# Branch projections of a decoder layer as seven block products each, with the weight sums formed earlier and kept in DRAM

## The chip, the cores and the metric

One NeuronCore of a Trainium2 chip. The metric is the device time of one execution in microseconds; lower is better. TensorE (PE) multiplies, VectorE (DVE) and ScalarE (ACT) work beside it, SyncE (SP) and ACT issue the DMAs, each on a queue of its own. Each engine takes its instructions in order; waits on semaphores order them against each other.

## What is computed

One layer, 512 tokens, width 2048, float32. A normalised h feeds one wide input projection; 8 heads of three branches (differential attention, dilated attention, gated convolution) give three y of 512 x 1024. Then:

```python
gates = sigmoid(h @ w_gates + gate_b)            # 512 x 3 x 2048
merged = (gates[:, :, 0] * (ya @ w_branch_a)     # each 512x1024 @ 1024x2048
          + gates[:, :, 1] * (yb @ w_branch_b)
          + gates[:, :, 2] * (yc @ w_branch_c))
x = x + merged @ w_out                           # 512x2048 @ 2048x2048
out = rmsnorm(x) * final_g
```

## The kernel before

**Precision.** Each operand of a product is split into a high part (ACT, a copy to a rounded type, `hi_of`, line 705 on) and a low part (DVE, the difference, `lo_of`, line 1017). A product is three matmuls: high x high, low x high, high x low (`three`, lines 419 to 423). The profile's lines L421, L422 and L423 are these three, L703 and L707 ACT's splits, L1015 and L1019 DVE's.

**Weight ring.** Weights come in units of 128 x 1024 floats (512 KB) through a ring of three slots (`raw`, `w_hi`, `w_lo`). SP loads a slot when DVE has split the unit before in it (`ring_free`); ACT splits a unit when TensorE has used the one three places back; DVE follows; TensorE waits for DVE (`lo_done`).

**Stages.** (1) The heads: 8 heads x 18 blocks x 2 units of 24 matmuls, with attention in between. Beside this, once per head, ACT loads four quarters of w_out into `ssum` (block 2), DVE forms the sums of quarters (block 7, `sum_out_units`, line 1049), ACT stores them to `s_dram` (block 8). (2) The gates: the projection of h to 6144 columns in 6 quads of 1024 columns. A quad is a 2 x 2 block product in seven products instead of eight: sums of weight quarters (`add_units`, DVE) against sums of quarters of h (`t1` to `t4`, made by `combine_h` in the last head and in the first quad, with `f1` to `f4` as temporaries of 128 x 2048). A product has 4 units of 12 matmuls; a quad 28 units. The seven products accumulate in three pairs of PSUM banks (`CHAIN`, `FRESH`); DVE takes each into its outputs with the right sign (`take_g`). The gates go to `g_dram`. (3) The branches: 12 groups (3 branches x 4 groups of 512 columns), each 4 units of 24 matmuls, an ordinary product in one of two sets of four banks (`sets`). `load_gates` brings the four gate tiles of a group, DVE multiplies them in and adds into `merged` (`take_group`, lines 1370 to 1384). y comes from `y_dram` by `load_y` (2 MB) and is split in four pieces (`high_y`, `low_y`). For the last branch, merged is transposed by TensorE (`turn_merged`, line 631) and copied by ACT (`copy_merged`, line 911) into `m_t`. (4) The output: 2 quads of seven products of 4 units, as in the gates; the weight sums come from `s_dram`, those of merged are made in the first quad (`g1f`, `g3f`, `g4f`), x is loaded into `res` (line 957), and `take_o` (line 1415) evicts onto it.

The places of all this side work are written out by hand: in each engine's program, `if n == ...` after the split of unit n.

```python
for n in range(NU):                      # branches, DVE, before (abridged)
    lo_of(R_B + NU * g + n, ...)
    if n == 2:
        take_group(g - 1)
```

Of the kernel before, what the change touches and what calls it, by code (L numbers as in the profile page):

```python
# [27 lines left out]
P = 128  # L28
D = 2048
# [29 lines left out]
GROUPS, NU = 12, 4  # L59
R_G = W1  # L60
R_B = R_G + QUADS_G * STEPS
R_O = R_B + GROUPS * NU
X_B = 8 * QUADS_G
X_O = X_B + GROUPS * NU
W11, W12, W21, W22 = range(4)
ON_X, ON_Z, ON_Y = range(3)
# [7 lines left out]
S_ORDER = [2, 3, 0, 1]  # L74
# [11 lines left out]
def spot(s):  # L86
    return S_ORDER.index(s)
# [16 lines left out]
def program(nc, wst, wg, wb, wo, x_t, x_tok, cols_d, rows_d, lam_d, const_d, out_d):  # L104
# [4 lines left out]
    s_dram = nc.dram_tensor("s_dram", (HEADS, 4, P, HU), f32, kind="Internal").ap()  # L109

    with ExitStack() as ctx:
# [74 lines left out]
        with ExitStack() as c2:  # L186
            s2 = sb_in(c2)
            s2("below2", [P, KT * T])
# [14 lines left out]
        def part(tile, n):  # L203
# [12 lines left out]
        y_parts = [[tile[:, 4096 * n:4096 * (n + 1)].rearrange("p (k q) -> p k q", k=8) for n in at]  # L216
                   for tile, at in ((tb, (0, 1)), (kb_r, (1, 2)))] + [[act_hi[:, 0:8, :], act_hi[:, 8:16, :]]]
        y_raw = kb[:, 0:4096].rearrange("p (k q) -> p k q", k=8)
        merged = act_lo_f[:, :, :].rearrange("p (s k) q -> p s (k q)", s=4)

        m_t = tb_f[:, 0:8192].rearrange("p (k q) -> p k q", k=KT)
        flat_hi = act_hi[:, :, :].rearrange("p k q -> p (k q)")
        flat_gin = gin[:, :, :].rearrange("p k q -> p (k q)")
        o11 = [part(tb, 4), part(tb, 5)]
        o_t1, o_t2, o_t4 = [[part(kb_r, n), part(kb_r, n + 1)] for n in (0, 2, 4)]
        o_t3 = [part(gin_r, n) for n in (0, 1)]
        o21, o22 = [[part(flat_hi, n), part(flat_hi, n + 1)] for n in (0, 2)]
        operands_o = [o11, o_t1, o_t2, o21, o_t3, o22, o_t4]
        g1f, g4f, g3f = part(kb, 3), part(kb, 5), part(flat_gin, 1)
        m11, m12 = [m_t[:, 0:8, h * H:(h + 1) * H] for h in range(2)]  # L230
        m21, m22 = [m_t[:, 8:16, h * H:(h + 1) * H] for h in range(2)]
        res = merged

# [5 lines left out]
        sets = [sc_ps + tr_ps, [o_ps] + pb]  # L239
# [8 lines left out]
        yraw_in, gin_in = sem("yraw_in"), [sem(f"gin_in{i}") for i in range(2)]  # L248
# [21 lines left out]
        yhi_done, ylo_done = sem("yhi_done"), sem("ylo_done")  # L270
# [20 lines left out]
        def _(sp):  # L291
# [49 lines left out]
            def load_gates(g):  # L341
                b, cg = divmod(g, 4)
                sp.dma_start(gin[:, 4 * (g % 2):4 * (g % 2) + 4, :],
                             g_dram[b, :, :, C * cg:C * (cg + 1)].rearrange("s p q -> p s q")).then_inc(gin_in[g % 2], 16)
# [28 lines left out]
            sp.wait_ge(ylo_done, 4)  # L373
            load_y(1)
            for g in range(GROUPS):
                for u in range(NU):
                    ring_free(X_B + NU * g + u)
                    load_ring(X_B + NU * g + u, wb[g, u, :, :])
                    if g < 2 and u == 3:
                        for n in range(4 * g, 4 * g + 4):  # L380
                            sp.wait_ge(g_stored[n], 16 * QUADS_G)
                        load_gates(g)
                    if g >= 2 and u == 2:
                        if g < 6:
                            sp.wait_ge(m_got, 4 * (g - 1))
                        else:
                            sp.wait_ge(m_added, 4 * (g - 5))
                        load_gates(g)
                    if g == 2 and u == 0:
                        sp.wait_ge(ylo_done, 8)  # L390
                        load_y(2)
                    if g == 3 and u == 0:
                        sp.dma_start(rows[:, :], rows_d[0:1, 3 * D:4 * D].to_broadcast([P, D])).then_inc(grow_in, 16)
            for q in range(QUADS_O):
                for n in range(STEPS):
                    p, u = divmod(n, NU)
                    x = X_O + STEPS * q + n
                    ring_free(x)
                    load_ring(x, wo[NU * q + u, (W11, None, None, W12, None, None, W22)[p], :, :] if p in (0, 3, 6) else
                              s_dram[NU * q + u, (None, W22, W11, None, W21, W12, None)[p], :, :])  # L400
# [15 lines left out]
        def _(pe):  # L416
# [176 lines left out]
            def product(r, operand, banks, p, free=None, between=None):  # L593

                hi, lo = operand
                for u in range(NU):
                    pe.wait_ge(lo_done, r + NU * p + u + 1)
                    slot = (r + NU * p + u) % RING
                    for s in range(2):
                        if free and u == 0:  # L600
                            pe.wait_ge(free[0], free[1][s])
                        for kk in range(2):
                            k, ts, cs = 2 * u + kk, slice(P * s, P * (s + 1)), slice(C * kk, C * (kk + 1))
                            end = three(banks[s][:, :], hi[:, k, ts], lo[:, k, ts], w_hi[slot][:, cs], w_lo[slot][:, cs],
                                        FRESH[p] and k == 0, k == 7, True)
                    end.then_inc(pe_used, 1)
                    if between:
                        between(u)
# [11 lines left out]
            for q in range(QUADS_G):  # L620
                for p in range(PRODUCTS):
                    if q == 0 and p in (1, 2, 4):
                        pe.wait_ge(comb_lo, {1: 1, 2: 2, 4: 4}[p])
                    product(R_G + STEPS * q, operands_g[p], pairs[(q + CHAIN[p]) % 3], p, free_g(q, p))

            def turn_merged(g, s):

                cg = g % 4
# [939 lines left out]
```

## Time and profile before

| | us |
|---|---|
| median of 3 runs (2642.91 to 2644.52) | 2642.93 |
| the profiled execution's own time | 2641.48 |
| its span | 2639.7 |
| TensorE busy / DVE busy / ACT busy | 2616.3 / 1554.9 / 866.8 |
| mean granted clock of TensorE | 0.997 |

Stages on TensorE, by the first matmul of each: heads from 8.8, gates from 1735.2, branches from 2203.3, output from 2469.9; the last matmul starts at 2628.6. "Busy" counts a matmul to its modelled end, and matmuls overlap; their rate is read from the starts.

### The profile page before, as it was taken

Reading aid. Unit: us, or ns where it says so; the run is one execution under the profiler, and the core shown is the slowest. Engines: PE = TensorE matmul, PEld = TensorE weight load, DVE = VectorE, ACT = ScalarE, POOL = GpSimd, SP = SyncE. Lnnn points to the kernel's source line nnn. Section 1 sums busy time; section 2 is a strip of 40 time slices with the busy share of each in tenths; the row PEclk is TensorE's granted clock in tenths of the full one; section 3 lists DMA queues with packets and bytes.
Section 4 is the critical chain, followed back from the end, with each engine's and each line's share of the span. In section 5 each row is a group of like instructions: output and inputs, shape, how many; then the busy total and the mean of one; then the engine's idle time right before and its main releaser. Section 6 shows DMA issues by size and latency. Waiting matters only on the chain.

```text
span 2639.7 us, 31265 instructions
## 1 busy us (share of the span) xinstructions
PE 2616.3 (99%) x12030; PEld 2162.5 (82%) x12030; DVE 1554.9 (59%) x1911; ACT 866.8 (33%) x1089; POOL 0.2 (0%) x4
## 2 busy tenths in 40 slices
PE   9999999999999999999999999999999999999998
PEld 7888888888888888888888888878888888888776
DVE  7653654554455455365455446798877784444775
ACT  6222332322222233232232223334444443212454
POOL 0000000000000000000000000000000000000000
PEclk9999999999999999999999999999999999999999
DMA  6333333332332432333334243435455436444565
GB/s 220 120 92 126 97 118 97 120 124 91 124 132 84 131 116 89 112 108 123 93 120 131 84 132 124 139 114 186 168 190 177 164 131 247 160 144 143 189 190 195
DMA packets 102825, 359.41 MB, mean 136 GB/s; under 512 B 10017, under 2 KB 10274, under 8 KB 100770
## 3 DMA queue, kind: packets, MB, share of 16 engines
q1 hardware_dynamic: 82352, 296.49, 34.2%
q10 hardware_dynamic: 20338, 60.89, 6.3%
q8 instruction: 113, 1.85, 0.3%
q14 instruction: 22, 0.18, 0.0%
HBM read 317.50 MB, written 39.85 MB: 135 GB/s over the span
## 4 chain that ended last, share of the span: by engine, by line
PE 95%; DVE 3%; DMA 1%; issue 1%; SPq 0%; ACT 0%; DVEq 0%; ACTq 0%
PE proj L421 22%; PE proj L423 22%; PE proj L422 22%; PE sc_ps L421 3%; PE sc_ps L422 3%; PE sc_ps L423 3%; PE tr_ps L421 3%; PE tr_ps L422 3%; PE tr_ps L423 3%; PE o_ps L422 2%; PE o_ps L423 2%; PE o_ps L421 2%; PE tr_ps L462 2%; PE sc_ps L454 1%; DVE w_lo L1019 1%; PE o_ps L507 1%
## 5 line engine op out<-in xcount | busy, mean ns | idle before, releaser
L421 PE MATMUL proj<-act_hi,w_hi 128*128 128x512 f32 x2304 | 908.1, 394 | 0.5 <-DVE stage L1146 0.2
L423 PE MATMUL proj<-act_hi,w_lo 128*128 128x512 f32 x2304 | 898.2, 390 | 0.0
L422 PE MATMUL proj<-act_lo,w_hi 128*128 128x512 f32 x2304 | 897.2, 389 | 0.0
L1015 DVE TENSOR_TENSOR w_lo<-raw,w_hi 128x1024 fp32r<-128x1024 f32 x288 | 352.7, 1225 | 396.4 <-ACT w_hi L703 395.9
L703 ACT ACTIVATE w_hi<-raw 128x1024 fp32r<-128x1024 f32 x288 | 304.6, 1058 | 837.3 <-PE proj L423 832.3
L423 PEld LDWEIGHTS proj<-act_hi,w_lo 128*128 128x128 f32 x2304 | 432.5, 188 | 91.4
L421 PEld LDWEIGHTS proj<-act_hi,w_hi 128*128 128x128 f32 x2304 | 432.8, 188 | 89.2 <-issue 1.1
L422 PEld LDWEIGHTS proj<-act_lo,w_hi 128*128 128x128 f32 x2304 | 433.0, 188 | 86.3
L1019 DVE TENSOR_TENSOR w_lo<-raw,w_hi 128x1024 fp32r<-128x1024 f32 x152 | 185.7, 1223 | 219.2 <-ACT w_hi L707 218.9
L707 ACT ACTIVATE w_hi<-raw 128x1024 fp32r<-128x1024 f32 x152 | 161.2, 1061 | 353.3 <-PE proj L423 149.9
L707 ACT ACTIVATE w_hi<-kb 128x1024 fp32r<-128x1024 f32 x120 | 127.2, 1061 | 185.8 <-PE proj L423 65.4
L1019 DVE TENSOR_TENSOR w_lo<-kb,w_hi 128x1024 fp32r<-128x1024 f32 x120 | 146.5, 1222 | 57.5 <-ACT w_hi L707 57.5
L770 ACT ACTIVATE sc<-sc,nmax 128x768 f32<-128x768 f32 (+4 forms) x96 | 65.5, 683 | 181.2 <-DVE nmax L1160 101.1
L1146 DVE TENSOR_TENSOR stage<-proj,rstd 128x512 f32<-128x512 f32 x40 | 27.6, 691 | 97.8 <-PE proj L423 97.8
L421 PE MATMUL tr_ps<-w_hi,act_hi 128*128 128x512 f32 x192 | 74.7, 389 | 0.0
L422 PE MATMUL tr_ps<-w_lo,act_hi 128*128 128x512 f32 x192 | 74.7, 389 | 0.0
L784 ACT ACTIVATE qk_hi<-stage 128x512 fp32r<-128x512 f32 x32 | 20.2, 632 | 150.1 <-DVE stage L1146 106.2
L421 PE MATMUL sc_ps<-w_hi,act_hi 128*128 128x512 f32 x160 | 63.0, 394 | 2.5 <-DVE w_lo L1019 2.5
L1144 DVE TENSOR_TENSOR stage<-proj,rstd 128x512 f32<-128x512 f32 x24 | 26.1, 1088 | 64.6 <-PE proj L423 64.6
L422 PE MATMUL sc_ps<-w_lo,act_hi 128*128 128x512 f32 x160 | 63.0, 394 | 0.0
L421 PE MATMUL sc_ps<-w_hi,tb 128*128 128x512 f32 x144 | 56.4, 392 | 1.5 <-issue 1.5
L421 PE MATMUL proj<-w_hi,act_hi 128*128 128x512 f32 x144 | 56.3, 391 | 1.2 <-DVE w_lo L1019 1.2
(297 smaller groups left out, 3354.5 us busy)
## 6 DMA issues: line engine op xcount, KB each, us to landing
raw<-wst SPq DMA_DIRECT2D x288, 512.0 KB, 3.5
raw<-wg SPq DMA_DIRECT2D x48, 512.0 KB, 4.0
raw<-wb SPq DMA_DIRECT2D x48, 512.0 KB, 3.6
kb<-wg SPq DMA_DIRECT2D x10, 2048.0 KB, 7.6
ssum<-wo ACTq DMA_DIRECT2D x8, 2048.0 KB, 10.5
s_dram<-ssum ACTq DMA_DIRECT2D x8, 2048.0 KB, 7.5
raw<-s_dram SPq DMA_DIRECT2D x32, 512.0 KB, 3.4
kb<-wg SPq DMA_DIRECT2D x24, 512.0 KB, 5.9
```

Of the source, the lines that this page charges most:

```text
L421: nc.tensor.matmul(out, w_h, a_h, start=first, stop=False, skip_group_check=shared)
L422: nc.tensor.matmul(out, w_h, a_l, start=False, stop=False, skip_group_check=shared)
L423: return nc.tensor.matmul(out, w_l, a_h, start=False, stop=last, skip_group_check=shared)
L454: end = nc.tensor.matmul(sc_ps[m][:, 0:n], q_part[AQ][rows, qs], k_part[AK][rows, 0:n], start=step == 0, stop=step == 2)
L462: end = nc.tensor.transpose(tr_ps[idx % 2][:, n * P:(n + 1) * P], tile, ident[:, :])
L507: nc.tensor.matmul(o_ps[:, c * P:(c + 1) * P], v_g[g][:, c, :], pt_g[:, g - 1, c, :], start=g == 1 and c == 0, stop=False)
L703: nc.scalar.activation(w_hi[slot_w][:, :], raw[slot_raw][:, :], ACT.Copy).then_inc(hi_done, 1)
L707: nc.scalar.activation(w_hi[r % RING][:, :], src, ACT.Copy).then_inc(hi_done, 1)
L770: end = nc.scalar.activation(tile[:, lo:hi], tile[:, lo:hi], ACT.Exp, scale=scale, bias=nmax[:, m:m + 1], accum_out=sums[:, m:m + 1])
L1015: tt(w_lo[slot_w][:, :], raw[slot_raw][:, :], w_hi[slot_w][:, :].bitcast(f32), ALU.subtract).then_inc(lo_done, 1)
L1019: tt(w_lo[r % RING][:, :], src, w_hi[r % RING][:, :].bitcast(f32), ALU.subtract).then_inc(lo_done, 1)
L1146: ins = tt(blk[w][:, :], pb[w % RING][:, :], rstd[:, :], ALU.mult)
```

## The change

- Branches: 6 quads (`QUADS_B`) of 1024 columns, each a 2 x 2 block product with seven products of 2 units of 12 matmuls (`STEPS_B` = 14 units), in the order P1, P2, P6, P5, P7, P3, P4 (`ORDER_B`), in the three bank pairs. The first use of an output is copied by ACT from PSUM to `parts` (`first_of`), the second added by DVE; then the gates are multiplied in and merged is added to (`finish`, `finish_last`, `gate`).
- y: seven operands per branch, four of them sums of quarters made by DVE (`sum_y`), each split into high and low. The loads of y stand at units 9 of quad 0 and 6 of quad 2.
- Weight sums for branches and output (20 in all, `SUMMED`) are formed in blocks 2, 7 and 10 of the heads 0 to 6 (head 0 without block 2), loads in blocks 1, 4, 9, stores in 3, 8, 11. Branch and output weights are one array `ws`.
- `load_gates` brings the two tiles of one output part, at units 5, 7, 9 and 12.
- The sums of h: `f1`, `f2` earlier in the last head, `f4` and a three-step `f3` in the first gate quad; two of the first weight sums in block 16.
- Output: `m_t` lies where act_hi was; merged parts of the last quads are transposed one at a time through the fourth bank pair; x is loaded at unit 7 instead of 6; the row of final_g during the output's first quad.

```diff
-GROUPS, NU = 12, 4
+QUADS_B, STEPS_B, NU = 6, 14, 4
+P1, P5, P6, P2, P7, P3, P4 = range(PRODUCTS)
+ORDER_B = [P1, P2, P6, P5, P7, P3, P4]
+SLOT = {0: 0, 3: 0, 1: 1, 2: 1}
+GATED = [0, 3, 1, 2]
+LOAD_AT, SUM_AT = {1: 0, 4: 1, 9: 2}, {2: 0, 7: 1, 10: 2}
...
@@ SP @@
-            sp.wait_ge(ylo_done, 4)
-            load_y(1)
...
+            for qb in range(QUADS_B):
+                for n in range(STEPS_B):
+                    load_unit(X_B + STEPS_B * qb + n, 2 * qb + n % 2, ORDER_B[n // 2])
+                    if qb == 0 and n == 0:
+                        load_gates(0, 0)
+                    if n == 5:
+                        load_gates(qb, 3)
+                    if n == 7:
+                        load_gates(qb, 1)
+                    if n == 9:
+                        load_gates(qb, 2)
+                    if n == 12 and qb < QUADS_B - 1:
+                        load_gates(qb + 1, 0)
+                    if (qb, n) == (0, 9):
+                        sp.wait_ge(ylo_done, 6)
+                        load_y(1)
+                    if (qb, n) == (2, 6):
+                        sp.wait_ge(ylo_done, 7 + 6)
+                        load_y(2)
...
@@ PE @@
+            def turn_merged(qb, d):
+                pair = qb % 2
+                for s in range(2):
+                    n = gated(qb - 4, d, s)
+                    pe.wait_ge(m_added, gated(qb - 2, d, s))
+                    if n > 2:
+                        pe.wait_ge(m_copied, n - 2)
...
+            for qb in range(QUADS_B):
+                for i, p in enumerate(ORDER_B):
+                    if qb % 2 == 0:
+                        pe.wait_ge(ylo_done, 7 * (qb // 2) + i + 1)
+                    product(R_B + STEPS_B * qb + 2 * i, operands_y[qb // 2][p], pairs[(QUADS_G + qb + CHAIN[p]) % 3], p,
+                            free_b(qb, p), turns_b(qb, 2 * i), 2)
+            def turns_o(u):
+                if u in (0, 1, 3):
+                    turn_merged(5, {0: 3, 1: 1, 3: 2}[u])
...
@@ ACT @@
+            FIRST_AT = {4: P1, 8: P6, 10: P5}
...
-                    if q == 0 and n in (5, 6):
...
-                    if q == 0 and n == 6:
+                    if q == 0 and n == 2:
+                        first_of(QUADS_B - 1, P4)
+                    if q == 0 and n in (4, 5, 7):
+                        copy_merged(5, {4: 3, 5: 1, 7: 2}[n])
+                    if q == 0 and n == 7:
                         for i in range(4):
...
@@ DVE @@
+            def finish(qb, p):
+                d, first, op = {P2: (0, P1, ALU.add), P7: (3, P5, ALU.subtract), P3: (1, P6, ALU.add)}[p]
+                dve.wait_ge(pe_used, RING + R_B + STEPS_B * qb + 2 * ORDER_B.index(p) + 2)
+                bank = pairs[(QUADS_G + qb + CHAIN[p]) % 3]
+                for s in range(2):
+                    dve.wait_ge(d_first, first_in(qb, first, s))
+                    tt(parts[2 * SLOT[d] + s], parts[2 * SLOT[d] + s], bank[s][:, :], op).then_inc(d_added, 1)
+                dve.wait_ge(d_added, added_in(qb, p, 1))
+                gate(qb, d)
...
+                    elif n == 0:
+                        finish(qb - 1, P3)
+                    elif n == 3:
+                        finish_last(qb - 1)
+                    if n == 6:
+                        finish(qb, P2)
+                    if n == 12:
+                        finish(qb, P7)
+                    if qb in (1, 3):
+                        b = (qb + 1) // 2
+                        if n in (1, 4, 5, 7):
+                            sum_y(b, (P5, P6, P7, P4)[(1, 4, 5, 7).index(n)])
+                        if n in (8, 9, 10, 11, 13):
+                            low_y(b, (8, 9, 10, 11, 13).index(n))
+                    if qb in (2, 4) and n in (1, 4):
+                        low_y(qb // 2, 5 if n == 1 else 6)
```

## Rows read from the trace of the kernel before

**Rows 1.** The page, part 1: busy us (share of the span) x instructions.
```profile
PE 2616.3 (99%) x12030; PEld 2162.5 (82%) x12030; DVE 1554.9 (59%) x1911; ACT 866.8 (33%) x1089; POOL 0.2 (0%) x4
```

**Rows 2.** Busy time of each engine in two stretches, first gates, then output.
```profile
core 0: us, PE busy (x) PEld busy (x) DVE busy (x) ACT busy (x) POOL busy (x), PEclk, DMA share, GB/s
1820.00:2120.00 300.00, 300.00 (x1325) 248.51 (x1324) 238.70 (x229) 132.39 (x140) 0.00 (x0) 1.00 0.50 172
...
2530.00:2620.00 90.00, 90.00 (x399) 74.53 (x398) 57.58 (x62) 41.14 (x53) 0.00 (x0) 1.00 0.62 194
```

**Rows 3.** TensorE's waits, longest first: us in total, times, longest us.
```profile
PE sc_ps L421 <- DVE act_lo_f L1415: 2.5, 1, 2.5
PE sc_ps L421 <- DVE w_lo L1019: 2.5, 1, 2.5
```

**Rows 4.** Last head and first gate quad: timeline of DVE, of TensorE, and a stretch.
```profile
1720.24 1.23 DVE L1015 TENSOR_TENSOR w_lo<-raw,w_hi 128x1024 fp32r<-128x1024 f32 x1 [5.99 <-ACT w_hi L703]
...
1730.37 4.63 DVE L1033 TENSOR_TENSOR kb<-kb 128x1024 f32<-128x1024 f32 x4
...
1747.10 0.63 PE L422 MATMUL sc_ps<-w_lo,act_hi 128*128 128x512 f32 x1
1747.52 0.63 PE L423 MATMUL sc_ps<-w_hi,act_lo 128*128 128x512 f32 x1
...
1735.20:1787.00 51.80, 46.91 (x188) 36.57 (x187) 50.85 (x44) 20.99 (x19) 0.00 (x0) 0.93 0.25 80
```

**Rows 5.** Busy time over the whole branch stage (columns as in rows 2).
```profile
2203.30:2469.90 266.60, 266.57 (x1201) 221.51 (x1202) 119.47 (x134) 70.83 (x74) 0.00 (x0) 1.00 0.48 162
```

**Rows 6.** Heads 4 and 5: timeline of DVE and ACT; DMA issues (KB, us to landing).
```profile
997.20 1.23 DVE L1015 TENSOR_TENSOR w_lo<-raw,w_hi 128x1024 fp32r<-128x1024 f32 x1 [2.67 <-ACT w_hi L703]
1001.55 0.69 DVE L1146 TENSOR_TENSOR stage<-proj,rstd 128x512 f32<-128x512 f32 x1 [3.12 <-PE proj L423]
...
1106.02 1.06 ACT L703 ACTIVATE w_hi<-raw 128x1024 fp32r<-128x1024 f32 x1 [3.13 <-PE proj L423]
...
1117.99 1.23 DVE L1015 TENSOR_TENSOR w_lo<-raw,w_hi 128x1024 fp32r<-128x1024 f32 x1 [2.37 <-ACT w_hi L703]
...
DMA to landing us min/median/max: 8.2/10.5/10.7
...
s_dram<-ssum ACTq DMA_DIRECT2D x8, 2048.0 KB, 7.5
```

**Rows 7.** Start of the branches: timelines of SP, ACT, DVE and TensorE.
```profile
2188.35 0.43 SPq L339 DMA_DIRECT2D kb<-y_dram  x1
2190.70 12.89 SPq L312 DMA_DIRECT2D raw<-wb  x4
...
2193.79 1.06 ACT L707 ACTIVATE w_hi<-raw 128x1024 fp32r<-128x1024 f32 x1 [1.66 <-PE proj L423]
2200.92 1.06 ACT L707 ACTIVATE w_hi<-raw 128x1024 fp32r<-128x1024 f32 x1 [6.06 <-DMA raw<-wb]
...
2202.01 1.22 DVE L1019 TENSOR_TENSOR w_lo<-raw,w_hi 128x1024 fp32r<-128x1024 f32 x1 [5.90 <-ACT w_hi L707]
...
2203.33 0.47 PE L421 MATMUL sc_ps<-w_hi,tb 128*128 128x512 f32 x1 [1.48 <-issue]
```

**Rows 8.** Branches: additions into merged on DVE; DMA issues of units and gates.
```profile
2317.14 2.49 DVE L1384 TENSOR_TENSOR act_lo_f<-act_lo_f,gin 128x512 f32<-128x512 f32 x4
...
raw<-wb SPq DMA_DIRECT2D x48, 512.0 KB, 3.6
...
gin<-g_dram SPq DMA_DIRECT2D x12, 1024.0 KB, 5.9
```

**Rows 9.** Output's start: two stretches, TensorE's timeline, landing of the four x loads.
```profile
2469.90:2530.00 60.10, 56.40 (x254) 45.62 (x253) 52.15 (x45) 33.30 (x33) 0.00 (x0) 1.00 0.65 227
...
2482.00:2502.00 20.00, 17.48 (x81) 14.26 (x80) 16.44 (x14) 10.95 (x10) 0.00 (x0) 1.00 0.98 377
...
2496.10 0.47 PE L421 MATMUL sc_ps<-w_hi,kb_r 128*128 128x512 f32 x1 [2.52 <-DVE act_lo_f L1415]
...
DMA to landing us min/median/max: 7.4/13.6/19.1
```

More of the change, by code:

```diff
@@ L232, in program @@
         res = merged
+        parts = [rows[:, C * n:C * (n + 1)] for n in range(4)]
         pb = [ctx.enter_context(nc.psum_tensor(f"proj{i}", [P, T], f32)) for i in range(RING)]
@@ L590, in _, with product @@
                 blocks(i, 0)
-            def product(r, operand, banks, p, free=None, between=None):
+            def product(r, operand, banks, p, free=None, after=None, nu=NU):
                 hi, lo = operand
-                for u in range(NU):
-                    pe.wait_ge(lo_done, r + NU * p + u + 1)
-                    slot = (r + NU * p + u) % RING
+                for u in range(nu):
+                    pe.wait_ge(lo_done, r + u + 1)
+                    slot = (r + u) % RING
                     for s in range(2):
@@ L621, in _ @@
                 for p in range(PRODUCTS):
[L622 to L628, printed above, removed]
-                pe.wait_ge(m_added, 4 * (g - 4) + spot(s) + 1)
-                for kk in range(4):
-                    end = nc.tensor.transpose(sets[g % 2][s][:, P * kk:P * (kk + 1)],
-                                              merged[:, s, C * cg + P * kk:C * cg + P * (kk + 1)], ident[:, :])
-                end.then_inc(m_turned, 1)
@@ new lines, in _ @@
+                    product(R_G + STEPS * q + NU * p, operands_g[p], pairs[(q + CHAIN[p]) % 3], p, free_g(q, p))
+            def turn_merged(qb, d):
[5 more added lines that the diff above has]
+                        pe.wait_ge(m_copied, n - 2)
+                    c0 = C * (2 * pair + d // 2)
+                    for kk in range(4):
+                        end = nc.tensor.transpose(pairs[3][s][:, P * kk:P * (kk + 1)],
+                                                  merged[:, 2 * (d % 2) + s, c0 + P * kk:c0 + P * (kk + 1)], ident[:, :])
+                    end.then_inc(m_turned, 1)
@@ L1378, in take_group, with gate @@
+            def gate(qb, d):
+                b, cg = qb // 2, 2 * (qb % 2) + d // 2
+                dve.wait_ge(gin_in[d], 16 * (qb + 1))
+                for s in range(2):
+                    to, tile = merged[:, 2 * (d % 2) + s, C * cg:C * (cg + 1)], gin[:, 2 * d + s, :]
+                    stt(to if b == 0 else tile, tile, 1.0, parts[2 * SLOT[d] + s], ALU.add, ALU.mult).then_inc(m_got, 1)
                 if b:
[L1379 to L1381 removed]
+                    for s in range(2):
+                        to, tile = merged[:, 2 * (d % 2) + s, C * cg:C * (cg + 1)], gin[:, 2 * d + s, :]
+                        dve.wait_ge(m_got, gated(qb, d, s))
```

468 lines of the change are left out of this document (251 added, 217 removed).

## The prediction

> **What bounds the kernel now.** I read the page first: TensorE is busy for 2616.3 us of a span of 2639.7 us, DVE for 1554.9, ACT for 866.8 [rows 1]. The profiled execution took 2641.48 us, 1.8 us more than its span and 1.45 us under the median of 2642.93; I sum against the execution and move the difference to the median. A busy TensorE need not be a fast one, so I took windows without a wait: the first of [rows 2] has 1325 matmuls in 300.00 us, a pitch of 0.2264 us (the 0.39 us of a row is latency, not rate). A unit of 12 matmuls is then 2.72 us, one of 24 is 5.43 us. The list of TensorE's waits is short; its two longest are 2.5 us each [rows 3]. So time falls only with fewer matmuls, if no other engine then holds TensorE up.
>
> How much room is there? The ring has three slots. ACT's split of a unit starts 0.2 us after the unit three places back has ended, DVE's split 1.1 us after ACT's (2200.92, 2202.01), and TensorE can begin 1.3 us after that (2203.33) [rows 7]. Of the two units between, 5.4 us, some 2.6 us are used and **2.8 us are left** when units have 12 matmuls; with 24 it is 8.3 us. DVE spends 1.14 us on 1024 elements (four in 4.63 [rows 4]); ACT's 128x1024 I take at 1.0.
>
> **The change, part by part.**
>
> 1. *Fewer matmuls.* A branch had 4 groups x 4 units x 24 = 384 matmuls; now 2 quads x 7 products x 2 units x 12 = 336. Three branches: 1152 less 1008 = 144, all 128x512. 144 x 0.2264 = **-32.6 us**. The transposes of the merged sum stay 64. The stage took 266.6 us for 1201 matmuls [rows 5], as the pitch says, so nothing else is hidden in it.
>
> 2. *Weight sums in the heads.* 20 in place of 8, each a load of 2 MB, four DVE adds (4.6 to 4.8 us together) and a store. Today's, in block 7, hold up no matmul: none of the waits lies in the heads [rows 3]. At block 10 they come behind the split at 997.20 and end at 1003.1; the eviction stood at 1001.55, so it and what follows slip 1.6 us, under 8.3. At block 2 they follow the split at 1117.99 and shift what is behind them as little. The load for block 2 is issued behind ACT's split at 1106.02 and lands at the worst in 10.7 us [rows 6], at 1116.9, 2.3 us early; that of block 9 stands equally far ahead of block 10's sums. The store before a load takes 7.5 us [rows 6] of the 10.9 that a block gives it. Cost taken **0**; bounds: nothing, and, if a load under the added 48 MB lands 8 us late, 1 to 2 us in each of 13 places.
>
> 3. *Sums of h, last head and first gate quad.* DVE is solid there from 1730.37 on (50.85 us of the window's 51.80 [rows 4]), and the window's 188 matmuls would do with 42.6: 9.2 us lost, some 3 of them to matmuls at twice the pitch (1747.10 to 1747.52; granted clock 0.93 in the window [rows 4]). The change takes two add units (2.3) and both operations on f4 (4.5) out of blocks 16 and 17, puts the adds into an idle DVE (5.99 us before 1720.24 [rows 4]), and brings f4 (two) and a third f3 operation back inside the quad, f4's last two at 17 and 20. Going instruction by instruction with 1.14, 2.2 (2048 wide) and 1.32 us (two evictions), TensorE waits 0.4 at unit 3, 1.9 at 4, 1.8 at 5, and 0.3 to 1.3 at 7, 9, 10, 12, 14 and 15: 8.3 us. **-1 us**, bounds -4 and +3.
>
> 4. *Start of the branches.* Today the 2 MB load of branch 2's y (2188.35) goes ahead of the first branch unit (2190.70), whose split starts at 2200.92 rather than one unit behind those at 2193.79, at 2196.5; TensorE idles 1.48 us [rows 7]. This load moves: **-1.5**.
>
> 5. *The two loads of y.* They now stand in the middle of quads 0 and 2, where units last 2.72 us. In [rows 7] the unit behind the y load was there 12.6 us after that load's issue (2188.35 to 2200.92). Counting from a quad's first matmul, SP issues the y load of quad 2 at 5.5 (after DVE's split 3), so unit 7 is there at 18.1, where ACT wants it at 2.72 x 5 + 0.2 = 13.8: 4.3 late, less 2.8 of room, 1.5. In quad 0 the load goes out at 14.1 behind a gate load (0.5 MB, about 1 us): unit 10 at 27.7 against 22.0, less 2.8: 2.9. I add 0.8 for the units that follow, whose room is spent: **+5.2**. Bounds: 0, if a unit lands in its usual 3.6 us [rows 8] all the same, and 9.
>
> 6. *DVE in the branches.* A quad lasts 38.1 us. Splits take 14 x 1.14 = 15.9. An operation on 128x512 takes 0.60 to 0.62 us (four in 2.49 [rows 8]): a finish is two adds, two gatings, two sums into merged and its waits, 3.8; three of these and the last (2.5) make 13.9. Quad 3 adds four sums and five low parts of y, 10.2: **40.0 in 38.1**. Split n can begin at 2.72(n - 2) + 1.3 and must by 2.72n - 1.3. From quad 3's split 6 at 13.0 the DVE queue has no gap: finish to 18.0, split 7 at 18.0 (0.3 late), then with sums and low parts split 9 at 22.6, 11 at 27.1, 12 at 29.4, finish to 34.4, split 13, a low part, split 0 of quad 4 at 36.6, finish(P3) to 41.6, and split 1 there, due at 39.5: **+2.1**. After it there is time. Quad 1 has no sums into merged (34.8) and passes. Quad 5 has g1f and two low parts, 2.2 us each, at units 10, 11 and 13: its split 13 begins at 34.7 (0.6 late), split 0 of the output stage at 38.0 (1.2 late in all), and split 1, behind finish(P3), at 43.0; both are counted in the next term. ACT has 14 splits and 7 high parts at 1.0 and 8 copies, taken at DVE's 0.6: 26 us of 38, room.
>
> 7. *Start of the output stage.* Today TensorE lost 4.5 us in it: 254 matmuls, 16 of them transposes (about 1.8), in 60.10 us, against 55.6; the largest piece is 2.52 us before 2496.10, on the eviction of the first product behind 2048-wide DVE work [rows 9]. In the new order the transpose of quad 5's part 1 follows unit 1, but its bank is emptied by ACT behind the split of unit 4, which waits for unit 1: 1.0 and two copies, 1.9 us of idle TensorE. The copies of part 2 move from unit 6 to 7, and behind them the x load and the split of the third operand. On that clock of quad 5 (stage due at 38.1): unit 0 at 39.3, unit 1 at 44.3, unit 2 at 49.7, unit 7 done at 66.9. ACT splits unit 7 at 58.8, copies, and has the third operand's high part at 63.4; DVE's low part 65.6, split 8 66.8, the next operand's low part 69.0, split 9 70.2, first eviction 71.5. Product 3 may start then, at 71.6; without any loss it would start at 38.1 + 8 x 2.72 + 2.6 for 24 transposes = 62.5. So 9.1 us are lost against today's 4.5 to 4.8: **+4.3**, bounds 0 and 8. The x load's first quarter took 7.4 us [rows 9]; issued at 59.5 it is there at 67, before DVE asks.
>
> 8. *Traffic.* Unit loads double to 193 GB/s, gates 55, y 18: 266 GB/s. The chip moved 377 GB/s over 20 us [rows 9], and the output stage runs at 194 with TensorE never idle, 90.00 us of 90 [rows 2]. **0** beyond term 5. The gate loads moved later are each issued four or more units (11 us) ahead of use, and took 5.9 us for twice the bytes [rows 8].
>
> Sum: -32.6 - 1 - 1.5 + 5.2 + 2.1 + 4.3 = **-23.5 us**; 2641.5 becomes 2618.0, the median 2642.9 becomes **2619**.
>
> **A rule beside this.** After one of the 2.5 us waits the matmuls from 1747.10 ran 0.42 us apart, the 1.2 GHz level; after 2.52 us at 2496.10 the stretch kept a granted clock of 1.00 [rows 4, 9]. Terms 5 to 7 make some six new waits of 1 to 3 us; a slow stretch costs 7 x 0.2 = 1.4 us by those rows.
> The Trainium skill (TensorE: Matmul & The Clock Gate, Part 1) says that activity is what holds the clock up and that idleness gives it back to half rate, which speaks against any change that breaks up an unbroken stream. By that rule all six waits would be followed by such a stretch; by the row at 2496.10, none.
>
> **Rivals.**
> A. *Nothing new is exposed.* The y loads hold nothing up and DVE keeps pace: terms 5 to 7 vanish, 2643 - 35 = 2608; with half of term 7, 2610. For it: DVE is busy for only 119.47 of today's 266.60 us of branches [rows 5]. Against: the quads' sums above. 0.15.
> B. *More waits than I see.* Late ring units, DVE lateness and the slow clock fall together: 6 x 1.4 = 8 us, or double terms 5 and 7: 2627 to 2632. For it: twice the load rate, 2.8 us of room. 0.2.
> C. *The branches become DMA-bound, slower than before.* 84 units of 0.52 MB, 12.6 MB of gates and 4.2 of y are 61 MB. If the queue sustained only the 194 GB/s of the output stage, the stage would take 314 us, 47 longer: about 2692. It decides below 236 GB/s (258 us). Against: 377 GB/s in [rows 9]. 0.04.
> D. *The products don't shrink*, or a loss about equal to the gain: within 0.2%. The loops give 84 units of 12. 0.03.
> The forecast has 0.58.
>
> **Numbers.** 0.2% is 5.3 us, about what a measurement of this kernel can tell from no change. Faster: forecast, A and B, 0.93; same 0.03; slower 0.04. The range runs from A's 2608, less 2 for the bound of term 3, to the greater part of B, 2630.
>
> **What would show it.** TensorE: 11886 matmuls, busy less by 28 to 33 us. By step: waits on a raw unit in quads 0 and 2; a wait on DVE's split in quad 4's first units; an idle of 2 us before a transpose early in the output stage, and one of about 5 us on the first output eviction; no wait at the branches' first unit; no new one in the heads. I am wrong if the heads show TensorE waiting on DVE or ACT on ssum, or if unit loads in the branches come over 5 us after issue throughout.

## The result and the profile after

The changed kernel takes **2630.11 us** (median of 4 runs, 2625.20 to 2632.15) against 2643.72 beside it: ratio 0.9945 [0.9928, 0.9963], 13.6 us less. Run again later it took 2629.85 against 2644.85, ratio 0.9945 [0.9928, 0.9961]. It is faster, as forecast, but by 14 us where the forecast said 23.5; 2630.11 lies at the far end of the range (2606 to 2630), 0.1 us past it. The two profiled executions differ by 9.3 us (2632.15 and 2641.48). The one of the changed kernel is the slowest of its four; the fastest took 2625.20 us at a mean granted clock of 0.997, the other three had 0.995.

In the changed kernel L464 to L466 are the three matmuls, L752 ACT's split, L1097 DVE's, L679 the transposes of merged, L983 ACT's copies of them, L1491 the adding of a branch product and L1544 the output's eviction; the variants below shift these numbers by a few lines. The page of the changed kernel, part 1, stands against [rows 1]:

```profile
PE 2593.7 (99%) x11886; PEld 2138.7 (81%) x11886; DVE 1700.2 (65%) x2053; ACT 936.7 (36%) x1182; POOL 0.2 (0%) x4
```

144 matmuls fewer, as the sum said, and TensorE's busy time is 22.6 us less, not 28 to 33. Stage by stage (the same windows as [rows 2], the first gate quad as in [rows 4], the branch stage as in [rows 5], the first 60 us of the output stage as in [rows 9]):

```profile
core 0: us, PE busy (x) PEld busy (x) DVE busy (x) ACT busy (x) POOL busy (x), PEclk, DMA share, GB/s
1820.00:2120.00 300.00, 300.00 (x1325) 248.41 (x1324) 238.82 (x229) 133.14 (x142) 0.00 (x0) 1.00 0.51 172
1738.60:1790.40 51.80, 45.92 (x191) 34.80 (x191) 50.29 (x43) 19.20 (x18) 0.00 (x0) 1.00 0.23 77
2204.40:2451.70 247.30, 238.49 (x1049) 194.77 (x1048) 200.71 (x222) 137.70 (x163) 0.00 (x0) 0.99 0.73 248
2451.70:2512.00 60.30, 52.57 (x223) 41.70 (x224) 46.81 (x41) 30.32 (x30) 0.00 (x0) 0.94 0.65 228
```

The gates run as before. The branch stage has 152 matmuls fewer than [rows 5] and is only 19.3 us shorter, not 34; the output's first 60 us hold 223 matmuls instead of 254. These are TensorE's waits from the branches on; the kernel before has two long ones there, 1.48 us ahead of the first branch unit [rows 7] and 2.52 us at the output's first eviction [rows 9]:

```profile
engine line waited for: us in total, times, longest us
PE tr_ps L464 <- DVE w_lo L1097: 5.2, 3, 3.7
PE sc_ps L464 <- DVE act_lo_f L1544: 4.0, 1, 4.0
PE sc_ps L464 <- DVE w_lo L1097: 2.8, 2, 2.5
PE proj L679 <- ACT act_hi_f L983: 2.0, 1, 2.0
PE o_ps L464 <- DVE w_lo L1097: 1.4, 2, 1.1
PE sc_ps L464 <- DVE rows L1491: 1.0, 1, 1.0
```

The waits are not the whole loss. Below is the timeline of TensorE in quad 0 of the branches, then two windows, one behind the wait there and one behind that of the first eviction:

```profile
2235.52 0.47 PE L464 MATMUL tr_ps<-w_hi,kb_r 128*128 128x512 f32 x1 [3.72 <-DVE w_lo L1097]
...
2237.14 0.63 PE L464 MATMUL tr_ps<-w_hi,kb_r 128*128 128x512 f32 x1
2237.57 0.63 PE L465 MATMUL tr_ps<-w_lo,kb_r 128*128 128x512 f32 x1
```
```profile
2235.50:2241.00 5.50, 5.48 (x17) 4.40 (x18) 4.85 (x6) 1.84 (x3) 0.00 (x0) 0.69 0.79 232
2484.90:2489.00 4.10, 4.09 (x12) 3.27 (x13) 2.79 (x4) 0.00 (x0) 0.00 (x0) 0.63 1.00 405
```

From 2236.74 eight matmuls start 0.43 us apart instead of 0.2264: the granted clock is at its 1.2 GHz level after the wait, and TensorE is busy at half the rate. Such a stretch costs 8 x 0.2 = 1.6 us, 1.65 with its ends, and there are four: behind the waits of 3.72, 2.50, 1.95 and 4.02 us.

To compare kernels I summed, over TensorE's timeline, what each start lies beyond 0.2267 us after the one before it, in groups of at least 0.3 us. "Gates" is the first gate quad, "quads" are the waits on ring units in quads 0 to 3 with what follows them, "DVE" what the branches lose to a late DVE, "output" begins with the last units of quad 5. The last but one column is the first matmul of the gate stage.

| | gates | quads | DVE | output | start of gates | median |
|---|---|---|---|---|---|---|
| before | 9.2 | 1.7 | 0 | 4.5 | 1735.2 | 2643.7 |
| after | 8.5 | 9.9 | 2.5 | 13.1 | 1738.7 | 2630.1 |
| after, again | 8.5 | 12.0 | 1.9 | 12.8 | 1735.6 | 2629.9 |
| y whole, on ACT's queue | 8.6 | 4.8 | 1.5 | 10.7 | 1738.2 | 2624.4 |
| y in two blocks | 8.5 | 3.5 | 2.1 | 11.1 | 1735.8 | 2622.1 |
| y in four pieces | 8.6 | 0 | 2.1 | 12.6 | 1735.6 | 2619.5 |
| + transposes later | | 1.7 | 2.0 | 9.7 | 1738.2 | 2616.0 |
| + eviction earlier | | 0.6 | 2.0 | 12.4 | 1735.9 | 2618.9 |
| + x taken apart | | 1.3 | 2.1 | 8.7 | 1736.8 | 2616.9 |
| + DVE relieved | | 1.3 | 4.2 | 11.2 | 1735.9 | 2620.2 |
| without the branches' weight sums | 8.5 | 13.4 | 1.5 | 12.0 | 1740.3 | 2629.5 |
| all that helped | 8.5 | 0.3 | 2.0 | 2.3 | 1735.9 | 2608.8 |

(The lines with + build each on the four pieces. The last column is the median of four runs, the others come from one profiled execution each. The medians stem from four measurements, the last three on three different chips, each beside the kernel before, whose own median went from 2643.4 to 2644.9; ratios below are to it, and their intervals reach 4 to 5 us either way, so differences of 3 us between variants are indications.) For the two profiled executions the table gives -32.6 for the matmuls, -0.7, +8.2, +2.5, +8.6 and +3.5 for the start, so -10.5; the spans differ by -9.4.

### The profile page after: what moved, and what is told of

It is laid out like the page before. It is cut to its first block, busy times and chain, and to the rows that moved or that the text cites. A ratio compares the mean times of both kernels' runs of the same rounds, so it can differ in the third digit from the quotient of the medians.

```text
span 2630.3 us, 31503 instructions
## 1 busy us (share of the span) xinstructions
PE 2593.7 (99%) x11886; PEld 2138.7 (81%) x11886; DVE 1700.2 (65%) x2053; ACT 936.7 (36%) x1182; POOL 0.2 (0%) x4
## 4 chain that ended last, share of the span: by engine, by line
PE 89%; DVE 5%; DMA 3%; ACT 1%; issue 1%; SPq 0%; ACTq 0%; DVEq 0%
PE proj L464 21%; PE proj L466 21%; PE proj L465 21%; PE tr_ps L464 3%; PE tr_ps L466 3%; PE tr_ps L465 3%; PE sc_ps L464 3%; PE sc_ps L466 3%; PE sc_ps L465 3%; DMA raw<-s_dram 2%; DVE w_lo L1097 2%; PE tr_ps L505 2%; PE o_ps L465 2%; PE o_ps L466 2%; PE o_ps L464 2%
## 5 line engine op out<-in xcount | busy, mean ns | idle before, releaser
L464 PE MATMUL proj<-act_hi,w_hi 128*128 128x512 f32 x2304 | 908.8, 394 | 0.2 <-DVE stage L1219 0.2
L466 PE MATMUL proj<-act_hi,w_lo 128*128 128x512 f32 x2304 | 899.0, 390 | 0.0
L748 ACT ACTIVATE w_hi<-raw 128x1024 fp32r<-128x1024 f32 x288 | 305.0, 1059 | 826.2 <-PE proj L466 819.9
L1093 DVE TENSOR_TENSOR w_lo<-raw,w_hi 128x1024 fp32r<-128x1024 f32 x288 | 352.6, 1224 | 375.9 <-ACT w_hi L748 374.5
L466 PEld LDWEIGHTS proj<-act_hi,w_lo 128*128 128x128 f32 x2304 | 432.8, 188 | 91.4
L464 PEld LDWEIGHTS proj<-act_hi,w_hi 128*128 128x128 f32 x2304 | 433.2, 188 | 88.7 <-issue 1.6
L1097 DVE TENSOR_TENSOR w_lo<-raw,w_hi 128x1024 fp32r<-128x1024 f32 x188 | 229.2, 1223 | 119.0 <-ACT w_hi L752 118.7
L752 ACT ACTIVATE w_hi<-raw 128x1024 fp32r<-128x1024 f32 x188 | 199.5, 1062 | 265.8 <-PE tr_ps L466 69.4
L752 ACT ACTIVATE w_hi<-kb 128x1024 fp32r<-128x1024 f32 x120 | 127.5, 1062 | 186.4 <-PE proj L466 66.7
L1097 DVE TENSOR_TENSOR w_lo<-kb,w_hi 128x1024 fp32r<-128x1024 f32 x120 | 146.8, 1224 | 51.8 <-ACT w_hi L752 51.7
L464 PE MATMUL sc_ps<-w_hi,tb 128*128 128x512 f32 x200 | 79.9, 399 | 4.3 <-DVE w_lo L1097 3.2
L464 PE MATMUL tr_ps<-w_hi,tb 128*128 128x512 f32 x200 | 78.5, 393 | 4.7 <-DVE w_lo L1097 4.6
L466 PE MATMUL sc_ps<-w_hi,tb 128*128 128x512 f32 x200 | 79.3, 396 | 0.0
L465 PE MATMUL sc_ps<-w_lo,tb 128*128 128x512 f32 x200 | 79.2, 396 | 0.0
L466 PE MATMUL tr_ps<-w_hi,tb 128*128 128x512 f32 x200 | 77.9, 389 | 0.0
L465 PE MATMUL tr_ps<-w_lo,tb 128*128 128x512 f32 x200 | 77.9, 389 | 0.0
```

What stands on the lines that cost most here:

```text
L464: nc.tensor.matmul(out, w_h, a_h, start=first, stop=False, skip_group_check=shared)
L465: nc.tensor.matmul(out, w_h, a_l, start=False, stop=False, skip_group_check=shared)
L466: return nc.tensor.matmul(out, w_l, a_h, start=False, stop=last, skip_group_check=shared)
L748: nc.scalar.activation(w_hi[slot_w][:, :], raw[slot_raw][:, :], ACT.Copy).then_inc(hi_done, 1)
L752: nc.scalar.activation(w_hi[r % RING][:, :], src, ACT.Copy).then_inc(hi_done, 1)
L1093: tt(w_lo[slot_w][:, :], raw[slot_raw][:, :], w_hi[slot_w][:, :].bitcast(f32), ALU.subtract).then_inc(lo_done, 1)
```

## Experiments

### The changed kernel again

No edit.

> The changed kernel, unaltered, beside three variants of it. Question: are the extra 3 us ahead of the gates (start of the gates at 1738.65 instead of 1735.2) and the four stretches at half the TensorE clock behind long waits (at 2236.74, 2308.46, 2462.13 and 2485.92) a property of the program, or of one execution? If of the program: gates start at 1738 to 1739 again, and the same four waits are each followed by some 8 matmuls at 0.43 us, 1.65 us lost each. If of the execution: the start lies near 1735.5 and some of the four stretches are missing. Median near 2630 either way.

Measured: 2629.85 us (2629.43 to 2632.81). The first 60 us of the first execution, and of this one:

```profile
0.00:60.00 60.00, 56.46 (x259) 46.93 (x260) 40.65 (x69) 35.17 (x53) 0.20 (x4) 0.97 0.54 193
```
```profile
0.00:60.00 60.00, 57.38 (x277) 47.19 (x278) 42.49 (x71) 36.98 (x56) 0.20 (x4) 1.00 0.56 198
```

The same program started its gates at 1738.65 once and at 1735.58 once: the 3 us ahead of the gates belong to the execution. What separates the two is a wait of TensorE near 40 us, on an early sum of DVE, and a slow stretch behind the longer one:

```profile
40.33 1.02 PE L577 MATMUL tr_ps<-ones,xacc 128*128 128x1 f32 x8 [1.53 <-DVE xacc L1151]
```
```profile
38.99 1.02 PE L577 MATMUL tr_ps<-ones,xacc 128*128 128x1 f32 x8 [0.30 <-DVE xacc L1151]
```

No part of the change makes it. The expectation had tied both questions together, and they came out apart: the four slow stretches came back at the same four waits, the first of them with some 13 slow matmuls instead of 8. In these two executions of one program they stand in the same places. How far that holds for a changed one, the run with ACT's queue shows.

### y of branches 1 and 2 in four pieces

The edits from here on are shown abridged.

```
-  if (qb, n) == (0, 9): load_y(1)        # 2 MB
-  if (qb, n) == (2, 6): load_y(2)
+  if n in (8, 10, 11, 13) and qb in (0, 2): load_y_part(1 + qb // 2, ...)   # 0.5 MB
-  wait_ge(yraw_in, 16 * (b + 1))
+  wait_ge(yraw_in, 16 * (4 * b + 1))
```

> The loads of y of branches 1 and 2, 2 MB each, are cut into four pieces of 0.5 MB, issued on SP's queue at units 8, 10, 11 and 13 of quads 0 and 2 instead of all at once at unit 9 of quad 0 and unit 6 of quad 2. Nothing else is changed. Theory (the load as one block holds up the ring's unit behind it, and the wait is paid twice, once as itself and once as a stretch at half the clock): the waits of 3.72 us (quad 0) and 2.50 us (quad 2) fall to under 0.5 us each and the half-clock stretches behind them (1.65 us each) go with them, so 8 to 9.5 us less than the changed kernel, about 2621. Rival 1 (the bytes themselves are the limit, the same 2 MB beside the ring's units): the waits are spread into several small ones with the same sum, and only the half-clock stretches may go: 0 to 3.3 us less. Rival 2 (the half clock has to do with something else than the wait ahead of it): the waits go, the slow stretches stay: 6 us less.

Measured: 2619.45 us (2618.53 to 2619.76), ratio 0.9902 [0.9885, 0.9918]; 10.4 us less than the changed kernel beside it. TensorE's waits in the branches, all of them:

```profile
engine line waited for: us in total, times, longest us
PE tr_ps L469 <- DVE w_lo L1102: 1.2, 1, 1.2
PE sc_ps L469 <- DVE w_lo L1102: 0.3, 1, 0.3
```

Theory held, rivals 1 and 2 fell: the same bytes, in pieces between the ring's units, cost TensorE nothing, and the slow stretches of these two places went with the waits. What is left are the two of DVE.

### y whole, but on ACT's queue

```
-  sp.dma_start(y_raw, ...)      # unit 9 of quad 0, unit 6 of quad 2
+  act.dma_start(y_raw, ...)     # behind ACT's unit 7 and unit 4
```

> The loads of y of branches 1 and 2 stay whole (2 MB) but are issued by ACT on its own queue, behind its high parts of unit 7 of quad 0 and unit 4 of quad 2, at about the same moments as before. If order within one queue is what delays the ring's unit (it may not pass the 2 MB in front of it), the unit lands in 4 to 7 us after its issue instead of 11.7 to 12.6, and the waits of 3.72 and 2.50 us on PE fall under 1 us: 5 to 9 us less than the changed kernel. If it is the bandwidth of the moment (both queues share the same engines) the waits stay within 1 us of what they are, and the time is the same within 3 us.

Measured: 2624.43 us (2622.01 to 2625.34), 5.4 us less than the changed kernel. The size fits the first reading, but not the rows. The wait in quad 0, in this kernel, and the windows behind it and behind the first eviction:

```profile
2234.24 0.47 PE L458 MATMUL tr_ps<-w_hi,kb_r 128*128 128x512 f32 x1 [2.92 <-DVE w_lo L1095]
```
```profile
2234.20:2239.70 5.50, 5.46 (x24) 4.55 (x25) 4.83 (x6) 2.25 (x3) 0.00 (x0) 1.00 0.83 272
2476.70:2481.00 4.30, 4.26 (x19) 3.54 (x20) 2.82 (x4) 0.00 (x0) 0.00 (x0) 1.00 1.01 407
```

The wait in quad 0 is 0.8 us shorter, not gone (quad 2 loses 1.7 us, where the changed kernel lost 2.7 and a slow stretch). Order in one queue would have had the unit land 4 to 7 us after its issue; it landed after 9.9 us, against 10.6 in the changed kernel. In its own queue the unit did pass the load (it landed at 2231.80, y at 2235.40), yet ACT could split it at 2231.83, against 2233.10, and of this gain 0.5 us are the earlier start of this execution and some may be the earlier issue of the load (2219.60, against 2221.45). So order is not the main cause, at least in quad 0; in quad 2, where the load went out 2.7 us earlier than before, the wait fell by more, from 2.50 to 1.01 us. What is left is that the load's bytes and the ring's share the same transfer engines. In the changed kernel's trace these have no room while the unit is awaited (slices of a fortieth of 2226 to 2233; the share of the 16 engines is 9 tenths or more throughout):

```profile
DMA  9999999999999999999999999999999999999999
...
DMA packets 1156, 2.83 MB, mean 404 GB/s; under 512 B 41, under 2 KB 41, under 8 KB 1156
```

The Trainium skill (DMA: Bandwidth & Descriptors, Where 436 GB/s comes from) puts the side of the HBM at some 358 GB/s for one core; these 404 GB/s are above it, and nearer to the 425 that the same page gives for a load of 16 MB with one core at work.
The same trace has 429 GB/s over 7 us (from 1706.2 us), under two loads of ACT in larger packets (10.7 KB on average, here 2.4).

Most of the 5.4 us is the clock: here no wait from the gates on is followed by a slow stretch, not even that of 3.66 us. The mean granted clocks of all four runs say the same, 0.997 to 0.998, against 0.995 to 0.996 in the changed kernel beside it. Why the clock stayed up in this kernel was not found.

### No weight sums for the branches

Leaves out 12 of the 20 sets of sums; the branch products that want a sum take the plain block.

```
-  if w in LOAD_AT and not last ...:   m = 3 * i + LOAD_AT[w] - 1
+  if (w == 4 or fresh and w == 9) and not last:   m = i + 1      # the output's 8 alone
-  load_ring(x, (s_dram if summed_ else ws)[i, kind, :, :])
+  load_ring(x, (s_dram if summed_ and i >= I_O else ws)[i, kind, :, :])
```

> Leaves out the weight sums of the branch projections (12 of the 20 sets that the heads load, sum and store: blocks 4 and 7 of each head for the output's sets alone, one more in head 0); the branch products that want a sum take the plain weight block in its place. The matmuls and ring loads of the branches stay as they are. Theory of the prediction (sums in the heads cost nothing, PE is never idle there): the start of the gates moves by under 0.5 us, and the time is that of the changed kernel within 2 us; if the extra 3 us ahead of the gates are due to the load at block 4 of head 0 or to DVE's sums, they go, and the time is 3 us less. Rival (the added traffic or the added DVE work holds PE up in small amounts over all the heads): the span of the heads falls by more than 3 us. 48 MB less traffic through the HBM in the heads is also the most that traffic could matter to the clock: the granted clock in the heads would rise above 0.99 if so.

Measured: 2629.47 us (2627.51 to 2635.10). The heads' stretch in the changed kernel and without the sums:

```profile
420.00:1710.00 1290.00, 1290.00 (x6040) 1066.99 (x6040) 723.28 (x977) 359.32 (x493) 0.00 (x0) 1.00 0.42 143
```
```profile
420.00:1710.00 1290.00, 1289.99 (x6040) 1066.79 (x6039) 677.53 (x937) 358.19 (x492) 0.00 (x0) 1.00 0.33 109
```

34 GB/s and 46 us of DVE less, and the same 6040 matmuls in 1290 us. The sums cost nothing in the heads, and the granted clock there is 1.00 with them and without. Between the same two matmuls, from 7300 ahead of the gates to the first of the gates, it is 1556.9 us in the kernel before (8 sets of sums), 1557.2 in the changed one (20) and 1557.4 without the twelve. The first gate quad, too, loses the same 8.5 us. The gates began at 1740.3, not within 0.5 us of 1738.65 as expected, by a longer slow stretch in the first 60 us; and the waits for y were 4.87 and 3.60 us here, longer than with the sums, in the slowest of the four runs (2635.10). For the branches the edit changes only the array from which the summed units are read; whether that or the execution makes the difference was not tested.

### The transposes a unit later

On top of the four pieces: `turns_o` at units 0, 2, 3 in place of 0, 1, 3.

> The kernel with the loads of y in four pieces (e1_y_parts, 2619.45 us), and the last three groups of transposes of the output's start asked for at units 0, 2 and 3 instead of 0, 1 and 3. Nothing else. Theory: the transposes at unit 1 wait for ACT's copy of the group before (2.0 us, with 0.95 us of half-clock matmuls behind it in that run, 1.65 in others), and a unit later the copy is done: both go, but the first eviction of the output is bound by DVE and the load of x, not by PE, so it comes when it came, and the 3 us are given back there as a longer wait for the first bank (4.0 becomes 6 to 7 us). Net 0 to 1 us. Rival: the wait at the first bank does not grow, since the copies on ACT move forward with PE: 2 to 3 us less, 2616.5.

Measured: 2616.01 us (2614.21 to 2620.16), ratio 0.9889 [0.9872, 0.9905]: 3.4 less than the four pieces, nearer to the rival. The wait before the transposes is gone, and the wait for the first bank grew from 3.98 to 4.23 us only; ACT's copies moved forward with TensorE. The two medians are from different chips, and the profiled execution (2620.16, the slowest of the four) has a late start and 1.7 us of losses in quad 0 that the four pieces did not show, so the size is good to a few microseconds at best: the interval of its ratio overlaps with that of the four pieces.

### The first eviction earlier

On top of the four pieces:

```
-  n == 8: comb_high(8, ...) / comb_low(8)      n == 9: take_o(0, P1)
+  n == 8: take_o(0, P1)                        n == 10: comb_high(8, ...) / comb_low(8)
```

> The kernel with the loads of y in four pieces (2619.45 us), and in the output's first quad ACT's and DVE's high and low parts of the operand of the fourth product moved from unit 8 to unit 10 (it is wanted at unit 12), the first eviction from unit 9 to unit 8. Theory (the first eviction is late because 2.3 us of DVE work stands ahead of it): it starts at about 2467.9 instead of 2471.2 on the trace's clock, PE's wait for the first bank falls from 4.0 us to 0.7 to 1, and the half-clock stretch behind it (1.7 us) goes: 3 to 5 us less. Rival (the load of x, four quarters of 1 MB issued just before, keeps back both the first quarter and the ring's unit that landed at 2477.4): the wait at the bank shrinks, but PE then stands 2 to 3 us at unit 11 for the low part of a unit that lands as late as before; net 1 to 3 us less.

Measured: 2618.94 us (2616.89 to 2622.55), 0.5 us less than the four pieces, which is no difference. TensorE's waits from 2436 on:

```profile
PE sc_ps L469 <- DVE w_lo L1102: 2.9, 2, 2.6
PE o_ps L469 <- DVE w_lo L1102: 2.6, 1, 2.6
PE proj L684 <- ACT act_hi_f L988: 2.0, 1, 2.0
...
PE sc_ps L469 <- DVE act_lo_f L1549: 0.5, 1, 0.5
```

The rival's mechanism, with less than its gain (1 to 3 us): the wait at the bank fell from 4.0 to 0.5 us and two of 2.6 us took its place. The first is on a unit that ACT got from its load at 2476.09, 9.4 us after its issue, while the quarters of x were arriving (the last two landed at 2476.40 and 2481.48). The second is on a low part that DVE began at 2486.19, behind two 2048-wide sums. A late eviction had been hiding a late load, and a backlog of DVE behind it.

### x taken apart

On top of the four pieces:

```
-  ACT, output, n == 7: four loads of 1 MB
+  ACT, branches' quad 5, n == 9 and n == 11: quarters 0 and 1
+  ACT, output, n == 8 and n == 14: quarters 2 and 3
-  DVE, n == 9: take_o(0, P1)
+  DVE, n == 7: take_o(0, P1), ahead of comb_low 7
```

> The kernel with the loads of y in four pieces (2619.45 us), and the load of x taken apart: its quarters for the output's first quad are issued by ACT at units 9 and 11 of the branches' last quad, the other two at units 8 and 14 of the output's first quad, instead of all four at its unit 7; the first eviction stands at unit 7 of DVE, ahead of a low part. Theory (x is what sets the first eviction and the ring's late units there): the wait of 4.0 us at the first bank, the half-clock stretch of 1.7 us behind it and the 2.2 us lost near 2490 fall to under 2 us together: 5 to 6 us less, about 2614. Rival (the early quarters of 1 MB hold up the ring's units in the branches' last quad as y did, since the transfer that matters is the same size as two ring units): new waits of 1 to 3 us near the end of the branches, net gain 2 to 4 us.

Measured: 2616.91 us (2615.89 to 2617.85), ratio 0.9893 [0.9877, 0.9910]: 2.5 less than the four pieces. TensorE's longest waits left:

```profile
PE o_ps L469 <- DVE w_lo L1106: 2.4, 2, 2.2
PE proj L684 <- ACT act_hi_f L988: 2.0, 1, 2.0
PE tr_ps L469 <- DVE w_lo L1106: 1.2, 1, 1.2
```

The wait at the bank is gone, and no new one stands at the end of the branches, so the early quarters hurt nothing: the rival's mechanism fell, though its size came out. What took the place is DVE: 2048-wide sums at 2476.86, 2480.19 and 2482.51 keep unit 13's low part back to 2484.72, 2.2 us of wait, with a slow stretch of 1.65 us behind.

### DVE relieved at the end of quad 3

On top of the four pieces: the first two sums of the third branch's y at units 11 and 13 of quad 2, y's pieces at units 7 to 10 there, one low part instead of two in quad 4.

> The kernel with the loads of y in four pieces (2619.45 us), and the sums and parts of y for the third branch begun earlier: y's pieces issued at units 7 to 10 of quad 2, the first two sums at units 11 and 13 of quad 2, the rest in quad 3, and one low part instead of two left in quad 4. The same work in all. Theory (DVE is behind by the end of quad 3, since it has 8 or 9 us more to do there than in quad 2): the 0.53 us lost near 2319 and the 1.57 us lost near 2355 to 2359 go: 1.5 to 2 us less. Rival (what is late there is the groups of merges themselves, 5 us of DVE work that stand together at the ends of products): the losses stay within 0.5 us. A third outcome: earlier loads of y stand against gate loads at units 7 and 9 and bring a wait of 1 us or more back in quad 2.

Measured: 2620.22 us (2619.01 to 2622.51), 0.8 more, which is no difference. The waits in the branches:

```profile
PE o_ps L474 <- DVE w_lo L1107: 1.2, 1, 1.2
PE sc_ps L474 <- DVE w_lo L1107: 1.2, 1, 1.2
PE tr_ps L474 <- DVE w_lo L1107: 0.8, 1, 0.8
```

Half right: the 1.5 us at quad 4's first units went, as DVE's backlog said, but 3.1 us are lost where quad 2 passes into quad 3, where the two sums now stand between the merges (0.5 there without the edit), and 1.1 in the middle of quad 3. The backlog is moved, not lowered, and it is paid where merges and sums meet.

### y in two blocks

> The changed kernel with y's loads of branches 1 and 2 as two blocks of 1 MB, at units 9 and 12 of quads 0 and 2. A dose between one block of 2 MB (2629.85 us) and four of 0.5 MB (2619.45). If PE's wait is what the block keeps the next ring unit back by, less a fixed slack of the ring, the waits of 3.7 and 2.5 us fall to under 1 us each (1 MB at 377 to 400 GB/s is 2.7 us less in front of the unit), and there is no half-clock stretch behind them: 2620 to 2622. If pieces help only because they lie far apart, the waits stay above 1.5 us, and the time lies near the middle, 2624 to 2626.

The edit is that of the four pieces with two of 1 MB, at units 9 and 12. Measured: 2622.12 us (2620.83 to 2626.20), at the edge of the expected band, though by half of the mechanism. Quad 2 has no wait above 0.4 us. In quad 0:

```profile
PE tr_ps L468 <- DVE w_lo L1101: 3.4, 2, 2.3
```

2.3 us where I had said under 1. SP issued there, from 2217.74 to 2224.11, two gate loads, both halves of y and three units, 4.5 MB in 6.4 us: at 404 GB/s that is over 11 us. So size alone does not decide; what fits the rows is that it counts how much is issued within the ring's reach, gate loads too. No run here moved a whole load to another place, or changed the pieces' places alone.

### All that helped

The four pieces, the transposes at 0, 2, 3, x taken apart, and DVE's second operation of the last operand's sum moved from unit 12 to 17.

> What helped, together: y's loads in four pieces, the transposes at units 0, 2 and 3, x's quarters taken apart with the first eviction at unit 7, and the second half of the last operand's sum on DVE moved from unit 12 to unit 17 (with its high and low part behind it). Expected from the ledgers of the single runs: 2619.45 less 3.4 (transposes) less 2.5 (x) less 1 to 2 (of the 4.05 us that stood near 2483 in e5_y_x_early, where DVE had 7 us of sums in a row): 2612, 31 to 33 us under the kernel before. If instead the waits at the output's start are one backlog of DVE that each edit only moves along, the three gains do not add, and it comes out at 2615 to 2617.

Measured: **2608.82 us** (2608.60 to 2610.38), ratio 0.9868 [0.9851, 0.9884]: 34.6 us under the kernel before beside it, and 21 under the change. It beats the 2612 expected, since no wait above 1.2 us is left after the gates, and no slow stretch. Its waits from the branches on:

```profile
engine line waited for: us in total, times, longest us
PE tr_ps L469 <- DVE w_lo L1106: 1.2, 1, 1.2
PE sc_ps L469 <- DVE rows L1500: 1.0, 1, 1.0
PE sc_ps L469 <- DVE w_lo L1106: 0.5, 2, 0.3
PE o_ps L469 <- DVE w_lo L1106: 0.3, 1, 0.3
```

## Why the prediction was right, and where it was short

The direction was right, and for the reason given. That 2630.11 falls at the edge of the range is owed to the range, which took in most of rival B, and not to the sum.

1. *Fewer matmuls* (-32.6): right. 11886 matmuls, and the version with almost no waits is 34.6 us faster, as rival A said of such a kernel (2608 to 2610); only it took three more edits to be one.
2. *Sums in the heads* (0): right, shown by the run without them.
3. *First gate quad* (-1): -0.7, but in other parts. Waits of 1.67 and 1.41 stand at units 4 and 5 (1.9 and 1.8 predicted). Before, 3.3 of the 9.2 us were two slow stretches; after, no wait is above 1.7 us and the stretch has a clock of 1.00. So the waits grew by some 2.6 us and the clock gave back 3.3.
4. *Start of the branches* (-1.5): right, the wait is gone.
5. *The y loads* (+5.2): mis-sized, measured 9.9 and 12.0. The place and the order were right: 3.72 us in quad 0 (2.9 said), 2.50 in quad 2 (1.5 said). With what stands beside them they lose 6.6 us, 1.4 more than said (in the second execution the waits are 4.24 and 2.90). The rest is the clock: two slow stretches of 1.65 us.
6. *DVE from quad 3 to 4* (+2.1): 2.5 and 1.9, at the units named.
7. *Start of the output* (+4.3): mis-sized, +8.6 and +8.3. Its pieces were 1.4 where 1.2 was said, 1.95 for the transposes (1.9), 4.2 with the wait for the eviction (4.7), and 2.2 in small ones, most of it near 2500 (1.3 was left for these): 9.8 us without the clock, where 9.1 was said. What the sum lacked is two slow stretches, 3.35 us. That DVE's order makes the eviction late was right (with it moved the wait fell from 4.0 to 0.5 us); what the term had no place for is that the load of x makes ring units late there, and that such a unit was waited for as soon as the eviction was early.
8. *Traffic* (0 beyond term 5): right on the average (248 GB/s in the branches); the moment of 404 GB/s was term 5's.

**The step that failed** is the choice beside the sum: from [rows 4] and [rows 9], one long wait with a slow stretch and one without, the sum took none. Four of the waits had one, 6.6 us. That is rival B's mechanism, at 4 x 1.65 rather than 6 x 1.4. The rule of the Trainium skill (TensorE: Matmul & The Clock Gate, Part 1), that idleness gives the clock back to half rate, agrees with these four waits; it does not agree with the 3.66 us in the run with ACT's queue. Of the 13.0 us between the -23.5 forecast and the -10.5 of the table, 6.6 are the clock, 3.5 the late start, which belongs to that one execution, and the remaining 2.9 the sizes of waits. Against the two pairs of medians the gap is 9.9 and 8.5 us.

## What to carry to other kernels

Cut a load that is larger than what a ring's slack covers into pieces of a unit's size and put them between the units, gate loads counted in; here the same bytes then cost nothing. When a stream of matmuls is to be broken by waits of 2 us and more, price each at itself plus half of one slow stretch below 3 us and the whole of it above 3.5; this is an estimate from the counts below, all of one kernel and its variants. And when an eviction is late, look for the load that it hides before moving it.

## What the runs showed of the chip

- *Waits and the clock.* In the twelve profiled executions (before, after and the ten runs) TensorE had, from the gates on, 12 waits of 3.6 to 4.9 us: 11 were followed within 2 us by a stretch at 1.2 GHz. Of 20 waits of 1.9 to 2.9 us, 10 were. Of those under 1.7 us, none. Before the gates it was otherwise: near 40 us, ahead of eight one-column matmuls, five executions had a wait of 1.53 to 1.56 us, and four of them a slow stretch behind it. The length alone does not decide: 1.95, 2.50 and 3.72 us had one, 3.66, 2.92 and 2.64 had none, 4.23 us had 14 slow matmuls, and the wait of 1.9 to 2.2 us before the transposes had one in four traces and none in five. What tells them apart was not found.
- *The moment's bandwidth.* 404 GB/s over 7 us with all 16 engines busy, 429 with larger packets. With the load on a second queue the ring's unit landed ahead of it, but still 9.9 us after its issue.
- *The start.* The same program began its gates at 1735.6 or 1738.7 us, by a wait of 0.30 or 1.53 us near 40 us and the slow stretch behind the longer one. The end of one trace is not good to better than 3 us.
- Open: the 8.5 us of the first gate quad, which no run here touched, and the 1.5 us of DVE at quad 4, which one try moved and did not lower.
